# A hybrid decoder step on one core: forget rows stacked in one strip and made in the convolution, queries padded earlier, modulation pieces in every second unit

## The chip, the cores and the metric

The kernel runs on one core of a Trainium2 chip. The metric is the device time of one execution in microseconds. Times of single instructions come from one profiled execution; they count from its first instruction.

## What is computed

One layer of a decoder for two groups: a prompt of 512 tokens and 8 running samples (one token each, 2048 past positions in a paged cache). From the reference, cut to what matters here:

```python
mod = silu(c) @ w_mod + b_mod                       # 6 x 1024 columns, for 9 rows c
sh1, sc1, g1, sh2, sc2, g2 = split(mod, 6)
h = rms(x) * (1 + sc1) + sh1
gq, gk, gv, gz, ga, gb, fq, fk, fv, ff = split(h @ w_in)
# gated delta: short causal convolution of gq, gk, gv, silu, chunked state update -> o_gdn
# forgetting attention, 8 heads x 64:
F = cumsum(log_sigmoid(ff + fox_fb))
s = q @ k.T * 64 ** -0.5 + F[q] - F[k]              # causal; samples: over cached pages too
o_fox = softmax(s) @ v
x = x + g1 * (concat(o_gdn, o_fox) @ w_out)
x = x + g2 * peer(rms(x) * (1 + sc2) + sh2)         # 16 of 16384 experts for each of 8 heads
y = rms(x) * final_norm_w
```

## The kernel before

All engines run programs of their own that meet at semaphores. The stages, with their times in the profile: the first four of twelve chunks of `w_mod` (to 80 us), the input projections (to 205), the convolution (205 to 290), the forgetting attention of the prompt in **units** (307 to 462), the first tile's gated-delta levels with the output projection (to 600), and the expert part (to the end), in which POOL gathers rows of `peer_uv`.

**Projections and keys.** Weight chunks of 2 MB go through a ring; from the fourth chunk on only two slots alternate. SP issues all loads and stores in one order that is written out by hand. `chunk(n)` waits for the last matmul of the chunk that had the slot before. Beside the projections, POOL multiplies the samples' cached keys with their queries (`key_product`, line 2291), in 32 groups of 1 MB, and DVE reduces them (`key_group`).

**The convolution** (lines 625 to 643). PE makes twelve blocks in three groups `gq`, `gk`, `gv`; ACT, DVE and PE turn each block back (`conv_back`). After the last, PE makes the forget rows: `forget_rows(i)` multiplies `LOGF` with triangles into a bank, 1, 2, 4 and 7 matmuls for the four tiles, and ACT (lines 1182 to 1187) copies them into four strips `FORGET[i]`, rows 0 to 7, that lie in `MV` and in `HT`. Then PE turns the tails of the convolution (`TAILI`, to DVE's `TAILO`) and the samples' log forget pages (`forget_turns`), and DVE makes the score of the samples' new key.

**Padding the queries.** Two heads share 128 partitions. `FQ` keeps the even heads and `FQO` the odd ones, the other 64 partitions zero. On POOL, behind the 32 key products, stand in this order: `sample_conv(0)` (the samples' convolution of one group, 7 steps on 8x512), two memsets of the strips, the copy of 64 partitions into `FQO`, two memsets of 64 partitions, then `sample_conv(1)` and `sample_conv(2)`. PE's unit 0 waits for all five of the strips' and queries' instructions.

**Units.** There are 34 steps u, for 8 heads x 4 query tiles. Unit u has on PE `fox_scores(u)` (three matmuls: keys, forget row spread by a column of `ident`, mask), `fox_turn(u - 1)`, `fox_values(u - 2)`; on DVE the maximum (1649), a copy (1657) and the scaling (1666); on ACT the exponential (1204). In chosen units stands more, from tables by unit:

- `MOD_AT = (2, 5, 8, 12, 15, 18, 21, 24)`: `mod_chunk` on PE (64 matmuls on a chunk of the ring) and `mod_row` on DVE (line 1483, four instructions).
- PE's `steps` and DVE's `between`: the forget sums of the pages (`forget_sums`, unit 1; `forget_after` with 15 additions on line 1738 and one on 1740), `sample_scores` (units 9; lines 1747, 1749, 1752), the softmax of the samples (units 10 to 17), the samples' delta state (`srule_...`, units 16, 19, 22, 25, 29, with long instructions on lines 1692, 1699 and 1705 and three products on POOL between them).
- From unit 18 on one group of cached values each (`sample_values(n)`, n = u - 18): four pages of 256 KB, in a rotation of three buffers.
- After unit 10 ACT applies SiLU to the samples' convolution (line 1208), which waits for all three of POOL's `sample_conv`.

**SP's order around the units** (lines 2498 to 2590). `sconv_load(0)`, chunk 11 (the fifth modulation chunk), `sconv_load(1)`, chunk 12, `sconv_load(2)`; each `sconv_load(g)` waits for `sample_conv(g - 1)`. Then the biases of pieces 4 and 5, the stores of the convolution's tails, the samples' new score and two loads. Then `next_mod(m)` for m = 4, 5, 6: it waits for the piece's rows, stores them, loads a bias and issues the chunk after next (m + 9). Then it waits for the SiLU of unit 10, stores its result, loads the samples' state, and goes through the steps z of `for z in range(LEVELS_END)`: `next_mod` at z = MOD_AT + 2 for the remaining pieces, and `value_pages(n)` three steps ahead of its use:

```python
numbers = page_numbers(n)          # four register loads, line 2439
...
cache_group("cache_v", 32 + n, numbers)
```

## Time and profile before

| | |
|---|---|
| median of 3 runs | 2075.9 us (2069.58 to 2078.93) |
| the profiled execution | 2079.02 us, its span 2077.1 us |
| mean granted clock of TensorE | 0.916 |
| busy: PE, DVE, ACT, POOL | 80%, 65%, 32%, 39% of the span |
| HBM read | 718.50 MB, 350 GB/s over the span |
| DMA share from 640 us to the end | 0.99 |

The busy shares are means over stages that differ. Which engine or queue sets the end has to be read from the stage in question: from the windows, then from the chain of waits, then from the timeline of the engine that the chain names. Line numbers in rows are those of the kernel before; 484 and 491 are PE's helpers for matmul and transpose, 2380 and 2385 are SP's for loads and stores, and 2439 is the read of a page number into a register.

### The profile page before, as it was taken

The numbers are of one execution on the slowest core, as the hardware profiler recorded it, in microseconds if no ns is written. First come the engines' busy times: TensorE is split into PE (matmuls) and PEld (weight loads), VectorE is DVE, ScalarE is ACT, GpSimd is POOL, SyncE is SP. The second block draws the span as 40 slices with busy tenths as digits, with TensorE's granted clock in tenths as the row PEclk, the third lists the DMA queues.
The fourth block names the chain that finished last, engine by engine and source line by source line (L and its number), as shares of the span: only waits on it lengthen the run. The fifth ranks groups of instructions, "written<-read, shape, count | busy, mean of one in ns | idle before, by whom it ended". The sixth has DMA issues, their size and how long they took to land.

```text
span 2077.1 us, 25939 instructions
## 1 busy us (share of the span) xinstructions
PE 1654.9 (80%) x8212; PEld 880.5 (42%) x8212; DVE 1353.7 (65%) x3075; ACT 669.0 (32%) x1956; POOL 809.3 (39%) x604
## 2 busy tenths in 40 slices
PE   6999988888887896766599676759978778977776
PEld 4546546546664453333255234325522443322232
DVE  4236866564458886756878665688857667676754
ACT  2111222211124453323345332344523333442332
POOL 0178672213004443334354343434424344444441
PEclk9999999887998998999799899989978998999999
DMA  8378645886579999999999999999999999999996
GB/s 297 108 256 278 230 151 153 308 280 207 170 261 414 404 415 414 413 414 421 411 378 420 414 414 414 421 409 390 421 392 352 417 419 392 422 422 422 421 417 284
DMA packets 168826, 729.20 MB, mean 351 GB/s; under 512 B 17622, under 2 KB 18471, under 8 KB 101987
## 3 DMA queue, kind: packets, MB, share of 16 engines
q0 software_dynamic: 75024, 545.82, 64.0%
q1 hardware_dynamic: 93666, 181.73, 25.4%
q8 instruction: 67, 1.10, 0.2%
q14 instruction: 69, 0.56, 0.1%
HBM read 718.50 MB, written 9.09 MB: 350 GB/s over the span
## 4 chain that ended last, share of the span: by engine, by line
PE 36%; DMA 30%; DVE 12%; issue 8%; POOL 6%; SPq 4%; ACT 4%; DVEq 0%; POOLq 0%; ACTq 0%
PE bank L484 35%; DMA R<-in_peer_uv,R 21%; DMA R<-in_w_out 4%; POOL MV L2291 3%; SPq L2380 3%; DVE R L2127 2%; DVE RING L2127 2%; DMA RING<-in_peer_uv,R 2%; DMA R<-in_peer_wq 2%; POOL R L2291 1%; SPq L2439 1%; ACT R L1348 1%; PE bank L491 1%; POOL R L2366 1%; DVE R L1912 1%
## 5 line engine op out<-in xcount | busy, mean ns | idle before, releaser
L2366 POOL DMA_INDIRECT RING<-in_peer_uv,R x390 | 439.9, 1128 | 712.6 <-PE bank L484 577.3
L484 PE MATMUL bank<-RING,R 128*64 128x512 f32 (+2 forms) x1560 | 514.8, 666 | 223.7 <-ACT R L1348 219.8
L2127 DVE SCALAR_TENSOR_TENSOR RING<-RING,MV 128x1024 f32<-128x1024 f32 x288 | 351.5, 1223 | 177.9 <-DMA RING<-in_peer_uv,R 169.1
L484 PE MATMUL bank<-R 128*128 128x128 f32 (+6 forms) x2216 | 396.7, 375 | 83.1 <-ACT R L1348 75.1
L484 PEld LDWEIGHTS bank<-R 128*128 128x128 f32 (+3 forms) x2216 | 260.7, 186 | 243.3 <-issue 235.7
L484 PEld LDWEIGHTS bank<-RING,R 128*64 128x64 f32 (+2 forms) x1560 | 156.4, 159 | 484.5 <-issue 472.5
L1358 ACT ACTIVATE R<-R 128x2 f32<-128x2 f32 x256 | 51.8, 202 | 716.0 <-DVE RING L2127 592.8
L2366 POOL DMA_INDIRECT R<-in_peer_uv,R x130 | 147.6, 1136 | 213.8 <-PE bank L484 196.8
L2127 DVE SCALAR_TENSOR_TENSOR R<-R,MV 128x1024 f32<-128x1024 f32 x96 | 117.6, 1225 | 58.0 <-DMA R<-in_peer_uv,R 56.5
L2127 DVE SCALAR_TENSOR_TENSOR RING<-RING,R 128x1024 f32<-128x1024 f32 x96 | 117.3, 1222 | 55.1 <-DMA RING<-in_peer_uv,R 50.6
L484 PEld LDWEIGHTS bank<-HT,R 128*128 128x128 f32 x1024 | 128.0, 202 | 56.3 <-issue 55.2
L484 PE MATMUL bank<-HT,R 128*128 128x128 f32 (+1 forms) x1024 | 139.2, 293 | 5.5 <-DMA R<-in_peer_wq 4.7
L484 PE MATMUL bank<-HT,RING 128*128 128x512 f32 x320 | 141.6, 600 | 0.0
L2291 POOL TENSOR_TENSOR MV<-MV,RING 128x2048 f32<-128x2048 f32 x22 | 99.3, 4528 | 89.5 <-DMA RING<-samp_d 56.6
L1365 ACT ACTIVATE R<-R 128x1 f32<-128x1 f32 x512 | 122.8, 287 | 8.4
L484 PE MATMUL bank<-R,HT 128*128 128x64 f32 (+4 forms) x320 | 103.8, 461 | 22.1 <-DMA R<-in_w_out 22.1
L484 PE MATMUL bank<-RING,HT 128*8 128x128 f32 (+5 forms) x768 | 106.7, 345 | 5.1 <-ACT HT L1098 3.7
L1348 ACT ACTIVATE R<-hide_q,R 128x64 f32<-128x64 f32 x384 | 109.7, 333 | 0.0
L484 PE MATMUL bank<-R,ident 128*128 128x512 f32 (+3 forms) x228 | 99.3, 537 | 0.1
L484 PEld LDWEIGHTS bank<-HT,RING 128*128 128x128 f32 x320 | 60.7, 193 | 72.4 <-issue 72.3
L484 PEld LDWEIGHTS bank<-RING,HT 128*8 128x8 f32 (+1 forms) x768 | 63.4, 139 | 45.5 <-issue 43.9
L484 PEld LDWEIGHTS bank<-R,HT 128*128 128x128 f32 (+1 forms) x320 | 49.0, 199 | 77.6 <-issue 74.5
(322 smaller groups left out, 1842.3 us busy)
## 6 DMA issues: line engine op xcount, KB each, us to landing
R<-in_peer_wq SPq DMA_DIRECT2D x16, 2048.0 KB, 28.6
RING<-in_w_mod SPq DMA_DIRECT2D x12, 2048.0 KB, 8.3
MV<-in_cache_k SPq DMA_DIRECT2D x88, 256.0 KB, 3.5
R<-in_cache_v SPq DMA_DIRECT2D x84, 256.0 KB, 3.7
R<-in_w_out SPq DMA_DIRECT2D x6, 2048.0 KB, 34.4
MV<-in_cache_v SPq DMA_DIRECT2D x44, 256.0 KB, 4.0
RING<-in_w_in SPq DMA_DIRECT2D x5, 2048.0 KB, 9.7
R<-in_cache_k SPq DMA_DIRECT2D x40, 256.0 KB, 3.7
```

Source lines behind the costliest of these rows:

```text
L484: i = nc.tensor.matmul(out, lhsT, rhs, start=start, stop=stop, **k)
L491: i = nc.tensor.transpose(out, in_, ident[0:n, 0:n])
L1348: A(dst[:, k % 4, :], ones_, ACT.Copy, scale=AG[:, n % 4, s_:s_ + 1]).then_inc(S("diagonal"), 1)
L1358: A(AG[:, n % 4, s_:s_ + 2], DOT[:, n % 4, s_:s_ + 2], ACT.Gelu).then_inc(S("gelu"), 1)
L1365: A(AG[:, n % 4, x:x + 1], AG[:, n % 4, x:x + 1], ACT.Copy, scale=gate).then_inc(S("weights"), 1)
L1912: V.tensor_tensor(M, AT, level[:, lv:lv + 1, :].to_broadcast([P, 4, P]), ALU.mult).then_inc(S(f"level{hb}"), 1)
L2127: V.scalar_tensor_tensor(u, u, 1.0, H2HIGH if s_ % 2 and n < PAIRED * PH else H2[n // PH % 2], ALU.mult, ALU.mult, accum_out=DOT[:, n % 4, ...
L2291: T(k, k, QB[:, n // 4 % 2:n // 4 % 2 + 1, :].to_broadcast([P, 4, 512]), ALU.mult).then_inc(S("kprod"), 1)
L2366: nc.gpsimd.indirect_dma_start(UV[g % UN], None, a["peer_uv"][0], bass.IndirectOffsetOnAxis(ap=idx, axis=0)).then_inc(S(f"uv_in{g % UN}"), 16)
L2380: sp.dma_start(dst, src, **k).then_inc(S(sem), 16)
L2439: return [sp.value_load(PTB[0:1, 4 * n + g:4 * n + g + 1], min_val=0, max_val=a["cache_k"].shape[1] - 1) for g in range(4)]
```

## The change

`FORGET` becomes one strip of 512 columns in `R2`; tile i has its eight rows at partitions 32 i to 32 i + 7, and the matmul that spreads them takes column 32 i + h of `ident`. POOL zeroes the strip at the very start. `PR`, which had that place, moves to the start of `HT`. `forget_rows` and the ACT copies move behind the group `gk`, inside the convolution. The copy of the odd queries moves from POOL to ACT, behind the last SiLU; POOL's two memsets of queries stand ahead of `sample_conv(0)`. The tails, the turn of the log forget pages, the new score and the forget sums' additions become entries of the tables, in units 0 to 8. The modulation pieces stand in units 1, 3, ..., 15. SP's order follows: chunk 12 ahead of `sconv_load(1)`, two groups of value pages ahead of piece 6, pieces 4 to 8 ahead of the wait for unit 10's SiLU.

```diff
-        FORGET = [MV[:, 2, 256:384], HFLAT[:, 256:512], MV[:, 2, 384:768], HFLAT[:, 512:1024]]
+        FORGET = R2[:, 8192:8704]
-        PR = part(R2, 8192, 1024, n=2, c=512)
+        PR = part(HFLAT, 0, 1024, n=2, c=512)
-        MOD_AT = (2, 5, 8, 12, 15, 18, 21, 24)
+        MOD_AT = (1, 3, 5, 7, 9, 11, 13, 15)
 # PE
                 if g == 0:
                     decay_sums()
+                if g == 1:
+                    for i in range(TILES):
+                        forget_rows(i)
             conv_back(10)
             conv_back(11)
-            for i in range(TILES):
-                forget_rows(i)
-            (tails turned here)
-            forget_turns()
-                    pe.wait_ge(S("fox_zero"), 5)
+                    pe.wait_ge(S("fox_zero"), 2)
-                mm(b[:, 0:w], ident[:, h:h + 1].to_broadcast([P, P]), FORGET[i][:, 0:w], False, False)
+                mm(b[:, 0:w], ident[:, 32 * i + h:32 * i + h + 1].to_broadcast([P, P]), FORGET[:, 0:w], False, False)
-            steps = {1: forget_sums, 10: sample_max_turn, 12: sample_max_spread, 16: sample_sums}
+            steps = {0: tail_turns, 1: forget_turns, 3: forget_sums, 10: sample_max_turn, 12: sample_max_spread, 16: sample_sums}
 # ACT, at g == 1, behind the three exponentials
+                    act.wait_ge(S("forget_cleared"), 1)
+                    for i in range(TILES):
+                        b = full_bank(act, ("frow", i))
+                        rows = slice(32 * i, 32 * i + 8)
+                        if i:
+                            A(FORGET[rows, 0:i * P], b[0:8, 0:i * P], ACT.Copy).then_inc(S("forget_cols"), 1)
+                            act.wait_ge(S("forget_cols"), i)
+                        A(FORGET[rows, i * P:(i + 1) * P], b[0:8, i * P:(i + 1) * P], ACT.Copy, scale=-1.0).then_inc(free(("frow", i)), 1)
             conv_silu(11)
+            A(FQO[64:P, :, :], FQ[64:P, :, :], ACT.Copy).then_inc(S("odd_queries"), 1)
             act.sem_inc(S("sample_ready"), 1)
-            (the copies of the forget rows)
 # DVE
-            between = {1: forget_after, 9: sample_scores, ...}
+            between = {0: tails_out, 1: forget_turned, 2: new_scores, 3: forget_after, 4: lambda: forget_pages(14, 12), 5: lambda: forget_pages(11, 9),
+                       6: lambda: forget_pages(8, 5), 7: lambda: forget_pages(4, 0), 8: forget_total, 9: sample_scores, ...}
 # POOL
+            nc.gpsimd.memset(FORGET, 0.0).then_inc(S("forget_cleared"), 1)
 ...
             for n_ in range(32):
                 key_product(n_)
+            job_done(pool, ("gv", 4))
+            pool.wait_ge(S("kprod"), 32)
+            nc.gpsimd.memset(FQO[0:64, :, :], 0.0).then_inc(S("fox_zero"), 1)
+            pool.wait_ge(S("odd_queries"), 1)
+            pool.wait_ge(S("fox_zero"), 1)
+            nc.gpsimd.memset(FQ[64:P, :, :], 0.0).then_inc(S("fox_zero"), 1)
+            pool.wait_ge(S("fox_zero"), 2)
             sample_conv(0)
-            (two memsets of strips, the copy and two memsets of queries)
             sample_conv(1)
             sample_conv(2)
 # SP
             sconv_load(0)
             chunk(11)
-            sconv_load(1)
             chunk(12)
-            sconv_load(2)
             sp.wait_ge(S("kred"), 32)
             bmod(4)
             bmod(5)
+            sconv_load(1)
 ...
+            next_mod(4)
             sp.wait_ge(S("new_score"), 1)
 ...
-            for m in range(4, 7):
+            next_mod(5)
+            sconv_load(2)
+            for n in range(2):
+                cache_group("cache_v", 32 + n, page_numbers(n))
+            for m in range(6, 9):
                 next_mod(m)
 ...
-                if z - 2 in MOD_AT[3:]:
+                if z - 2 in MOD_AT[5:]:
```

## Rows read from the trace of the kernel before

**Rows 1.** Windows by stage: PE, PEld, DVE, ACT, POOL busy, clock, DMA share, GB/s

```profile
205.00:290.00 85.00, 85.00 (x406) 42.12 (x408) 65.98 (x77) 25.06 (x56) 49.55 (x12) 1.00 0.62 201
...
367.00:450.00 83.00, 68.27 (x587) 43.53 (x579) 50.14 (x101) 13.91 (x37) 21.15 (x3) 0.86 0.91 315
...
450.00:640.00 190.00, 152.41 (x960) 113.47 (x957) 92.07 (x206) 39.51 (x77) 30.05 (x25) 0.84 0.66 230
...
640.00:2077.00 1437.00, 1108.02 (x4665) 531.31 (x4663) 1010.55 (x2472) 540.28 (x1677) 577.39 (x510) 0.92 0.99 405
```

**Rows 2.** The chain of waits from 280 to 440 us

```profile
by line: SPq L2380 20.2%; issue 15.2%; SPq L2439 14.0%; PE bank L484 11.5%; SPq L2385 5.9%; POOL MV L2291 5.7%; DMA R<-in_cache_v 4.4%; PE bank L491 3.9%; DVE RING L1738 3.8%; POOL R L2299 2.4%; POOL R L2300 2.4%; DVE RING L1740 1.4%; ACT R
...
352.37 1.49 ACT R L1208
...
382.67 0.39 SPq L2380
```

**Rows 3.** The timeline around the last convolution, POOL then PE; start, duration

```profile
291.02 1.26 POOL L2297 TENSOR_TENSOR R<-R 8x512 f32<-8x512 f32 x1
...
300.50 0.53 POOL L2308 MEMSET MV<- 128x512 f32 x1 [0.22 <-POOL R L2300]
...
305.65 1.80 POOL L2316 MEMSET R<- 64x2048 f32 x1
...
307.55 0.46 PE L484 MATMUL bank<-R 128*128 128x128 f32 x2 [2.58 <-issue]
```

**Rows 4.** The timeline there, ACT and PE

```profile
291.77 0.63 ACT L1159 ACTIVATE R<-R 128x512 f32<-128x512 f32 x1 [0.25 <-ACT R L1117]
...
293.04 0.39 PE L484 MATMUL bank<-upper,small 128*8 128x128 f32 x2
...
293.26 0.38 PE L484 MATMUL bank<-lower,small 128*8 128x128 f32 x2
```

**Rows 5.** SP's timeline, 308 to 441 us

```profile
316.88 0.68 SPq L2380 DMA_DIRECT2D R<-in_state_conv  x1
...
374.42 1.89 SPq L2380 DMA_DIRECT2D R<-in_cache_v  x4
...
376.35 1.44 SPq L2385 DMA_DIRECT2D mod_d<-MV  x4
...
379.27 0.40 SPq L2380 DMA_DIRECT2D RING<-in_w_mod  x1
...
431.96 2.00 SPq L2380 DMA_DIRECT2D R<-in_cache_v  x4
```

**Rows 6.** SP's instructions of line 2439; ns min/median/max

```profile
L2439 SPq TENSOR_LOAD <-RQ x64: 260/266/1261, 366.9 to 451.3; - x64
```

**Rows 7.** DMA issues in three windows; last number: median us to landing

```profile
RING<-in_w_mod SPq DMA_DIRECT2D x8, 2048.0 KB, 8.2
...
R<-in_cache_v SPq DMA_DIRECT2D x4, 256.0 KB, 3.4
...
R<-in_cache_v SPq DMA_DIRECT2D x4, 256.0 KB, 6.3
```

**Rows 8.** PE's timeline, 360 to 445 us

```profile
366.87 1.93 PE L484 MATMUL bank<-RING,small 128*9 128x128 f32 x64
...
440.73 1.94 PE L484 MATMUL bank<-R,RING 128*32 128x512 f32 x8 [4.14 <-DMA R<-in_cache_v]
```

**Rows 9.** DVE: line 1738 (ns min/median/max), then its timeline

```profile
L1738 DVE TENSOR_TENSOR RING<-RING x15: 267/275/1362, 316.0 to 321.0; 128x64 f32<-128x64 f32 x15
...
346.04 1.22 DVE L1747 TENSOR_TENSOR RING<-RING 128x1024 f32<-128x1024 f32 x1
...
403.05 7.12 DVE L1692 TENSOR_REDUCE R<-R 64x64 f32<-64x4096 f32 x1
...
420.32 4.47 DVE L1699 SCALAR_TENSOR_TENSOR R<-R,small 64x4096 f32<-64x4096 f32 x1
...
436.82 7.04 DVE L1705 TENSOR_REDUCE R<-R 64x64 f32<-64x4096 f32 x1
```

More of the change, by code:

```diff
@@ L635, in _, with tail_turns @@
                     decay_sums()
+                if g == 1:
+                    for i in range(TILES):
+                        forget_rows(i)
             conv_back(10)
             conv_back(11)
-            for i in range(TILES):
-                forget_rows(i)
-            pe.wait_ge(S("tails"), 12)
-            for q in range(3):
-                b = take_bank(("tail", q), "D")
-                for j in range(4):
-                    tr(b[0:3, j * P:(j + 1) * P], TAILI[:, q * 4 + j, :], full(("tail", q)) if j == 3 else None)
+            def tail_turns():
+                pe.wait_ge(S("tails"), 12)
+                for q in range(3):
+                    b = take_bank(("tail", q), "D")
+                    for j in range(4):
+                        tr(b[0:3, j * P:(j + 1) * P], TAILI[:, q * 4 + j, :], full(("tail", q)) if j == 3 else None)
             def forget_turns():
@@ L1632, in _, with tails_out, new_scores @@
             conv_tokens(11)
-            for q in range(3):
-                b = full_bank(dve, ("tail", q))
-                V.tensor_copy(TAILO[0:3, q * 512:(q + 1) * 512], b[0:3, :]).then_inc(S("tail_out"), 1)
-                dve.wait_ge(S("tail_out"), q + 1)
-                dve.sem_inc(free(("tail", q)), 1)
-            dve.wait_ge(S("sample_ready"), 1)
-            T8 = CACC[0:NB, 0, :]
-            dve.wait_ge(S("decays"), 3)
-            step(V.scalar_tensor_tensor(small[:, 786:818], small[:, 300:332], -1.0, small[:, 690:722], ALU.mult, ALU.mult))
-            step(V.tensor_tensor(T8, PS[0:NB, COL_FQ:COL_FQ + 512], PS[0:NB, COL_FK:COL_FK + 512], ALU.mult))
-            settle()
-            V.tensor_reduce(SN[0:NB, :], T8.rearrange("p (h d) -> p h d", h=8), AXX, ALU.add).then_inc(S("new_score"), 1)
+            def tails_out():
+                for q in range(3):
+                    b = full_bank(dve, ("tail", q))
+                    V.tensor_copy(TAILO[0:3, q * 512:(q + 1) * 512], b[0:3, :]).then_inc(S("tail_out"), 1)
+                    dve.wait_ge(S("tail_out"), q + 1)
+                    dve.sem_inc(free(("tail", q)), 1)
+            def new_scores():
+                dve.wait_ge(S("sample_ready"), 1)
+                T8 = CACC[0:NB, 0, :]
+                dve.wait_ge(S("decays"), 3)
+                step(V.scalar_tensor_tensor(small[:, 786:818], small[:, 300:332], -1.0, small[:, 690:722], ALU.mult, ALU.mult))
+                step(V.tensor_tensor(T8, PS[0:NB, COL_FQ:COL_FQ + 512], PS[0:NB, COL_FK:COL_FK + 512], ALU.mult))
+                settle()
+                V.tensor_reduce(SN[0:NB, :], T8.rearrange("p (h d) -> p h d", h=8), AXX, ALU.add).then_inc(S("new_score"), 1)
             def fox_max(u):
@@ L1736, in forget_after, with forget_pages, forget_total @@
                     job_read(dve, ("ltot", half))
-                for g in range(14, -1, -1):
+            def forget_pages(last, first):
+                for g in range(last, first - 1, -1):
+                    settle()
                     step(V.tensor_tensor(TP[:, :, :, g], TP[:, :, :, g], TP[:, :, :, g + 1], ALU.add))
-                    settle()
+            def forget_total():
+                settle()
                 step(V.tensor_tensor(flat(LP[:, :, :, 0:15]), flat(LP[:, :, :, 0:15]), flat(TP[:, :, :, 1:16]), ALU.add))
@@ L2512, in _, with next_mod @@
             store(o["conv_prompt"][0, 0], TAILO[0:3, :], "samples_out")
+            def next_mod(m):
+                mod_store(m)
+                if m + 2 < 12:
+                    bmod(m + 2)
+                chunk(m + 9)
+            next_mod(4)
             sp.wait_ge(S("new_score"), 1)
@@ L2552, in value_pages @@
                 b, q = divmod(n, 4)
-                numbers = page_numbers(n)
+                if n >= 2:
+                    numbers = page_numbers(n)
                 if buffer_of(32 + n) == 3 and group_before(32 + n) is None:
@@ L2558, in value_pages @@
                     sp.wait_ge(S("values_read"), before_ - 32 + 1)
-                cache_group("cache_v", 32 + n, numbers)
+                if n >= 2:
+                    cache_group("cache_v", 32 + n, numbers)
                 if q == 0:
```

27 lines of the change are left out of this document (1 added, 26 removed).

## The prediction

> **What bounds the kernel now.** I read the busy time by stage first [rows 1]. The last 1437 us, from 640 on, have a DMA share of 0.99 at 405 GB/s: expert rows and weights stream there and nothing in the change touches them, so a gain made earlier is handed down whole and no more. In the convolution (205 to 290) PE is busy all 85 us at full clock (1.00, the 2.4 GHz level). In the units of forgetting attention neither PE nor DVE is full (68 and 50 of 83 us from 367 on, clock 0.86) [rows 1], so something else sets the pace there.
>
> The chain of waits names it [rows 2]: SP's own instructions are the largest part between 280 and 440 (20.2% and 14.0% for the two lines that issue loads and read page numbers). It enters SP from the SiLU of the samples' convolution, which ACT does in unit 10 and ends at 353.9; from there SP issues without a pause to speak of up to the pages of unit 29, issued at 431.96 [rows 5], for which PE then waits until 440.73 [rows 8]. The kernel's middle is thus a serial list of SP. The way into it is the second thing to look at: POOL works 9.3 us on the first sample convolution, then until 307.45 on zeroing and copying, and unit 0 starts only at 307.55 [rows 3].
>
> **Part 1, the start of the units.** The forget rows move into the convolution. Pairs of passes start 0.22 us apart at full clock (293.04, 293.26) [rows 4]; 14 pairs are 3.1 us on an engine that is full, so the convolution ends at 293.4 in place of 290.3. The seven small ACT copies fall into gaps of some 6 us that ACT has there and cost nothing; without those gaps they would cost 0.3 us each. The last SiLU moves from 291.77 [rows 4] to 294.9 and ends at 295.5. Behind it stands ACT's new copy of half the queries, 64x2048. No such instruction exists before: a floor is ACT's 8x1536 at 1.49 us [rows 2], a ceiling is POOL's 64x2048 memset at 1.80 [rows 3] scaled up by a third; both say 1.5 to 2.4, I take 1.9, as 1.49 grows to 1.98 with the length. To 297.4, then POOL's second memset, 1.80, to 299.2. The first runs beside ACT. Unit 0 starts at 299.4: **8.2 us earlier**. The turns of the tails and of the forget pages now stand behind scores in units 0 and 1, in the shadow of waits for ACT's first table.
>
> **Part 2, what SP must do before the SiLU.** POOL's first sample convolution, in front of the queries before, is now behind them: 299.2 to 308.5. SP stands at the second group's load for exactly that. Its list from there, from its own rows [rows 5, 6]: the load of state and weights, 0.68 for the first of its two DMAs, 1.2 in all; three stores at the same rate, 1.6; the first modulation piece, stores, bias and chunk, 3.3 as from 376.35 to 379.67, to 314.6; the new score's store, some 2 of waiting for it (an estimate, not below 1 and not above 3) and two loads, 3.8; second piece 3.3 to 321.6; wait for POOL's second group to 323, load 1.2; two groups of value pages, each four register loads of 0.27 plus 0.15 and a gap, 2.6 together, and 1.89 of issues: 9.0, to 333.2; third and fourth piece 6.4, to 339.6. A chunk of 2 MB lands 8.2 us after its issue [rows 7]. The piece of unit 5 (issued 314.2, landed 322.4) costs 1 or 2 us, that of unit 7 none, but that of **unit 9** is issued at 336.0 and lands at 344.2, where PE could have been there at 336. PE's 1.93 [rows 8], DVE's rows to 347.5, then the three passes of sample scores (1.22 each, 3.8) [rows 9], the maximum, the exponential, ACT's table and SiLU of 2.8: it ends at **355.5 against 353.9**. The 8.2 us of the earlier start are eaten by SP's list.
>
> **Part 3, from the SiLU to the pages.** SP's stores and state loads are as before, 9.4, then one piece, 3.3: chunk issued at 367.7, landed 375.9, used in unit 15. Piece 10 (1.85, no bias any more) fits below it. PE arrives in unit 15 at 366 and waits till 375.9; its rows are done at 379.1, SP's last piece to 381, page numbers 2.6: the third group of values is issued at 383.6 against 382.67 before [rows 2]. So here the change is 1 us **behind**. What it gained, two groups out of the list (9.0) and two pieces, went into the wait for that chunk.
>
> **Part 4, behind unit 20.** Before, three pieces stood among the nine page groups from 382.67 to 431.96 [rows 2, 5]: 3.3, and 1.85 for each of the two without a bias, together 7.0. Now none: 9 x 4.5 + 0.7 = 41.2 against 49.3, so the group of unit 29 is issued at 424.8, 7.2 earlier. It also lands sooner: behind a chunk a group takes 6.3 from issue to landing, alone 3.4 [rows 7]. PE gets it at 430 in place of 440.73. PE and DVE now come into play: nine units with values are about 33 us of PE, and of DVE's state reduction of 7.1 in unit 22 and update of 4.5 in unit 25 [rows 9] some 7 stick out, as PE's gaps around them do now, so 432 to 433. **Net 8 us less.** Unit 30, the rest of the units, the levels and the gather stage follow it; the page groups of the levels wait on values read and move along.
>
> **Sum:** -8 us at the end of the units, against the profiled execution's own 2079.02: 2071. The median shown, 2075.9, lies 3.1 below that execution, so for the median I say 2075.9 - 8 = 2068. This main case has its own range of -3 to -13: the 1.5 to 2.4 of the copy, the landing times (7.8 to 9 us a chunk), and PE's clock, which is 0.84 in the stretch from 450 on [rows 1], after waits, and may do so after the new ones in units 9 and 15. A measurement of this kernel can tell about 0.5%, 10.4 us, from no change.
>
> **POOL beside DVE.** The forget sums' 15 additions are 0.275 us at the median but 1.362 at most [rows 9]; the long ones are those beside one of POOL's passes of 1.26 [rows 3]. Before they fell into a gap of POOL's; in units 4 to 8 they lie beside its second and third sample convolution. The Trainium skill (SBUF - State Buffer, Who interferes with whom) says that a DVE instruction with two SBUF inputs blocks against a GpSimd one that reads SBUF, whole instruction against whole instruction; the trace agrees. By it all 15 would take the long form. By the rows that is 15 x 1.09 = 16 us more on DVE, against none; I take half, since POOL rests between its groups, and put it under the wait for the chunk of unit 9, where DVE has 8 us. If all of it came, some 5 us would stick out and the main case would be -3. That is a rival of its own with 0.08.
>
> **Rivals.** *The front holds its gain* (0.22): SP reaches the chunk of unit 9 early enough, say because POOL's groups end sooner. The SiLU then ends near 343, and all shifts by a further 12: -20, 2056. For it: SP stands behind POOL at both loads, before (the one at 316.88 [rows 5] follows the end of POOL's second group at once) and after, so whatever POOL gains counts. Against it: the sum of SP's rows leaves it 1.6 us of waiting only.
>
> *The back is not SP's* (0.12), the slower side. The samples' state chain is a ladder of DVE and POOL steps tied to the units 16 to 32, with DVE's long ones at 403.05, 420.32 and 436.82 [rows 9]. From unit 15's piece (366.87 [rows 8]) to the end of the last of them, 443.9, it takes 77 us. The piece now waits for its chunk until 375.9, 9 later. If the 77 us stay, because the ladder and not the pages paced the units, unit 29 ends at 453, and with 3 of doubled collisions the kernel is +12: 2088. It decides if unit 15's piece to the end of unit 29's reduction still takes over 70 us. Against it: the three long DVE steps are 18.6 us of it, and PE's largest single waits are for value pages.
>
> *The change does nothing* (0.08): each gain is met by the next wait, within 2 us. The ring of two slots would then be the rate all through.
>
> **How the numbers follow.** Main case 0.50, of which a fifth lies beyond -10.4; the front's gain 0.22; nothing 0.08; collisions 0.08; the ladder 0.12, three quarters of it beyond +10.4. Faster: 0.10 + 0.22 = 0.32, rounded up to 0.33, as the front may win in part. Slower 0.09. Same 0.58. The range reaches from the front's gain, 2056, to a little over the case of nothing, 2079; what is left out is the ladder and the tail of the front.
>
> **What would show it.** Unit 0's scores at 299.4; a PE wait for a w_mod load of some 8 us in unit 9 and of 10 in unit 15; the SiLU's end near 355; third value group at 383.6; PE's wait in unit 29 for cached values, 4.14 us before [rows 8], gone or short; no piece on SP behind 381. Wrong if those ring waits are absent (front) or if the 77 us from unit 15 to unit 29 stay (ladder).

## The result and the profile after

The changed kernel takes 2085.1 us (median of 20 runs, 2077.8 to 2096.1), the kernel before 2076.8 (20 runs, 2068.9 to 2086.3). The ratio is 1.0037 with an interval of 1.0024 to 1.0050: slower by 0.4%, within the 0.5% that the prediction called no change, but outside its range, which ended at 2079, and on the other side of the forecast of 8 us less. The profiled execution spans 2084.5 us, 7.4 more than that of before. Three executions far above all others, one each of the kernel before (2173.9), e3_pieces_old (2364.8) and e6_no_chunks (5161.5), stand in no ratio.

The windows by stage (columns as in [rows 1]) show where to look:

```profile
205.00:290.00 85.00, 84.67 (x367) 42.05 (x366) 59.23 (x69) 23.17 (x55) 47.66 (x12) 1.00 0.60 193
299.00:308.00 9.00, 9.00 (x97) 7.26 (x98) 5.11 (x12) 2.31 (x5) 8.53 (x7) 0.68 0.15 52
308.00:367.00 59.00, 42.26 (x471) 31.55 (x470) 37.77 (x93) 10.45 (x23) 17.87 (x15) 0.86 0.68 226
367.00:450.00 83.00, 67.29 (x501) 44.20 (x499) 50.07 (x100) 15.82 (x42) 21.14 (x3) 0.94 0.79 258
```

For the stretch from 308 to 367 the kernel before has this row:

```profile
308.00:367.00 59.00, 48.78 (x472) 37.28 (x473) 38.96 (x100) 15.23 (x35) 17.91 (x14) 0.91 0.51 157
```

PE is busy all 9 us from 299 to 308 (6.25 of them before). Then it loses 6.5 us of busy time in the next 59, while the DMAs move more (226 GB/s against 157). So the start is earned and then lost. PE's timeline says at which instructions (start, duration, wait before it and what ended it):

```profile
299.00 0.77 PE L484 MATMUL bank<-R 128*128 128x128 f32 x2 [3.19 <-issue]
...
322.09 1.94 PE L484 MATMUL bank<-RING,small 128*9 128x128 f32 x64
...
336.09 3.28 PE L484 MATMUL bank<-RING,small 128*9 128x128 f32 x64 [7.25 <-DMA RING<-in_w_mod]
...
347.56 0.47 PE L491 MATMUL bank<-ident,HT 128*128 128x128 f32 x1 [5.13 <-ACT HT L1209]
...
349.56 3.37 PE L484 MATMUL bank<-RING,small 128*9 128x128 f32 x64
...
384.00 3.21 PE L484 MATMUL bank<-RING,small 128*9 128x128 f32 x64 [5.38 <-DMA RING<-in_w_mod]
```

The pieces are the rows with `RING,small`. Those of units 5, 7, 9 and 15 stand here. The one of unit 7 waits 7.25 us for its chunk and that of unit 15 waits 5.38. Both then take 3.2 to 3.3 us instead of 1.94, at a granted clock of 0.56 and 0.58 (1.00 for the piece of unit 5). The piece of unit 9 takes 3.4 us, behind PE's wait of 5.13 for ACT.

SP's timeline shows why the chunk of unit 7 was late:

```profile
314.36 0.40 SPq L2393 DMA_DIRECT2D RING<-in_w_mod  x1
314.82 0.45 SPq L2398 DMA_DIRECT2D sgate_d<-RQ  x1
...
322.14 0.36 SPq L2393 DMA_DIRECT2D RQ<-out_logf_sample  x1
...
326.35 0.39 SPq L2393 DMA_DIRECT2D RING<-in_w_mod  x1
326.78 0.70 SPq L2393 DMA_DIRECT2D R<-in_state_conv  x1
...
339.98 0.40 SPq L2393 DMA_DIRECT2D RING<-in_w_mod  x1
343.64 0.40 SPq L2393 DMA_DIRECT2D RING<-in_w_mod  x1
...
375.96 0.52 SPq L2393 DMA_DIRECT2D RING<-in_w_mod  x1
...
392.99 2.00 SPq L2393 DMA_DIRECT2D R<-in_cache_v  x4
...
433.78 1.93 SPq L2393 DMA_DIRECT2D R<-in_cache_v  x4
```

The chain of waits shows how long the chunk of unit 7 then took to land:

```profile
326.35 9.70 DMA RING<-in_w_mod
```

SP's waits from 290 to 460 (total, times, longest) give the same list by cause:

```profile
SPq L2398 <- DVE MV L1488: 19.4, 4, 10.2
SPq L2393 <- DMA sgate_d<-RQ: 6.8, 1, 6.8
```

The first is SP waiting for the rows of a piece (`MV`). They wait for PE, and PE waits for the chunk, so a delay goes round. But not all of it is the ring's: ahead of unit 9's piece PE waits 5.13 us for ACT, which comes behind five additions of the forget sums on DVE (5.81 us). The second is the store of the new score, 0.2 KB, issued at 314.82 right behind the 2 MB of the chunk at 314.36.

The chain of waits from 280 to 440, by line, has turned over against [rows 2]:

```profile
by line: PE bank L484 52.5%; DMA RING<-in_w_mod 11.1%; PE bank L491 7.4%; issue 5.6%; DVE R L1702 4.4%; DVE MV L1488 4.2%; DVE RING L1752 2.8%; DVE R L1709 2.2%; DVE HT L1667 0.9%; DVE RING L1791 0.8%; DVE RING L1779 0.8%; DVE RQ L1785 0.8%
```

SP's issues and register loads, a third of the chain before, are gone from it. In their place stand PE and the loads of `w_mod`. The SiLU and the last long step of DVE:

```profile
360.95 1.48 ACT L1213 ACTIVATE R<-R 8x1536 f32<-8x1536 f32 x1
...
442.64 7.09 DVE L1715 TENSOR_REDUCE R<-R 64x64 f32<-64x4096 f32 x1
```

The SiLU ends at 362.4 (353.9 before), the third value group is issued at 392.99 (382.67, both [rows 2]), the reduction of unit 29 starts at 442.64 (436.82 [rows 9]). At the end of the units DVE's first memset of the levels marks the time, before, then after:

```profile
460.48 0.48 DVE L1843 MEMSET R<- 128x512 f32 x1 [0.35 <-DVE R L1809]
```

```profile
464.12 0.48 DVE L1861 MEMSET R<- 128x512 f32 x1 [0.35 <-DVE R L1826]
```

The loss of 10.3 us at 393 has shrunk to 3.6 there. The first expert gather is issued at 623.78 against 618.53.

### The profile page after: what moved, and what is told of

Its sections match the earlier page's. It is cut to its first block, busy times and chain, and to the rows that moved or that the text cites. A ratio compares the mean times of both kernels' runs of the same rounds, so it can differ in the third digit from the quotient of the medians.

```text
span 2084.5 us, 25938 instructions
## 1 busy us (share of the span) xinstructions
PE 1667.9 (80%) x8212; PEld 881.3 (42%) x8212; DVE 1348.2 (65%) x3075; ACT 670.8 (32%) x1957; POOL 805.8 (39%) x602
## 4 chain that ended last, share of the span: by engine, by line
PE 46%; DMA 29%; DVE 15%; issue 4%; ACT 4%; POOL 1%; SPq 1%; DVEq 0%; ACTq 0%; POOLq 0%
PE bank L484 44%; DMA R<-in_peer_uv,R 17%; DMA R<-in_w_out 6%; DMA RING<-in_peer_uv,R 5%; DVE RING L2145 3%; DVE R L2145 2%; DMA RING<-in_w_mod 2%; PE bank L491 2%; ACT R L1353 1%; SPq L2393 1%; POOL R L2379 1%; DVE R L1930 1%; ACT R L1363 1%; ACT R L1370 0%; DVE R L1919 0%
## 5 line engine op out<-in xcount | busy, mean ns | idle before, releaser
L484 PE MATMUL bank<-R 128*128 128x128 f32 (+6 forms) x2216 | 406.3, 382 | 87.6 <-ACT R L1353 78.0
L484 PE MATMUL bank<-R,ident 128*128 128x512 f32 (+5 forms) x292 | 125.1, 526 | 0.1
```

Of the source, the lines that this page charges most:

```text
L484: i = nc.tensor.matmul(out, lhsT, rhs, start=start, stop=stop, **k)
```

## The experiments

All ratios are to the kernel before, on the same chip and in the same hours: over 20 runs of each for the change, and over 7 to 12 runs against 18 to 35 of the kernel before for the others. The landmarks are those of one profiled execution of each kernel. "Units' end" is the start of the memset just named. The times of the landmarks:

| kernel | ratio (interval) | SiLU ends | third value group | units' end | first gather |
|---|---|---|---|---|---|
| before | 1 | 353.9 | 382.7 | 460.5 | 618.5 |
| the change | 1.0037 (1.0024 to 1.0050) | 362.4 | 393.0 | 464.1 | 623.8 |
| e1_store_first | 1.0013 (0.9994 to 1.0033) | 360.9 | 392.5 | 463.9 | 620.6 |
| e2_pages_in_loop | 1.0028 (1.0010 to 1.0047) | 362.3 | 393.3 | 467.6 | 620.4 |
| e3_pieces_old | 0.9954 (0.9935 to 0.9974) | 348.2 | 373.3 | 450.4 | 601.1 |
| e4_adds_by_6 | 1.0024 (1.0007 to 1.0042) | 362.1 | 393.3 | 464.6 | 621.2 |
| e5_small_first | 0.9930 (0.9906 to 0.9954) | 347.9 | 371.0 | 450.1 | 600.5 |
| e6_no_chunks | 0.9936 (0.9911 to 0.9961) | 354.2 | 380.0 | 450.5 | 607.2 |
| e7_old_pages_in_loop | 0.9971 (0.9952 to 0.9990) | 349.6 | 378.4 | 458.1 | 609.3 |
| e8_mid_pieces | 0.9977 (0.9958 to 0.9996) | 355.9 | 376.1 | 459.2 | 619.7 |
| e9_small_adds | 0.9962 (0.9943 to 0.9981) | 349.8 | 375.0 | 452.8 | 606.3 |
| e10_conv_first | 0.9973 (0.9956 to 0.9991) | 355.2 | 377.8 | 457.6 | 615.2 |
| e11_old_store_first | 0.9967 (0.9949 to 0.9984) | 349.7 | 374.1 | 453.8 | 604.4 |
| e12_small_again | 0.9953 (0.9933 to 0.9972) | 347.7 | 370.9 | 449.6 | 607.3 |

**e1_store_first.** The new score's store and its two loads go ahead of piece 4's chunk.

```diff
-            next_mod(4)
             sp.wait_ge(S("new_score"), 1)
...
+            next_mod(4)
             next_mod(5)
```

> Edit: the changed kernel, with SP's fifth modulation piece (its row stores, bias and 2 MB chunk) moved from ahead of the new score's store to behind the two loads that wait for that store. In the changed kernel SP stands 6.8 us for this store, which was issued 0.4 us behind the chunk. Theory 1 (SP's list and the queue order starve the ring): the wait falls to some 2 us, the next chunk is issued near 321.5 instead of 326.35, PE's wait of 7.3 us in unit 7 shrinks to under 3, the SiLU of unit 10 ends near 357 instead of 362.4, and the time falls by 3 to 6 us against the changed kernel (about 2080, ratio to the kernel before 1.001). Theory 2 (the units are longer because PE and DVE have more work in each, the ring is incidental): the SiLU stays within 1.5 us of 362.4 and the time does not move. Theory 3 (DVE's additions beside POOL): POOL's third group starts near 327 instead of 337 and the additions of unit 7 escape it, so part of the gain is that.

Measured: 2082.6 us against 2079.3. The wait of 6.8 is down to 0.3. But two chunks are now issued in a row, at 317.85 and 321.46, with the loads of `sample_conv` and eight value pages behind them, and they take 9.0 and 11.7 us to land. PE pays one piece earlier, in unit 5:

```profile
326.86 3.60 PE L484 MATMUL bank<-RING,small 128*9 128x128 f32 x64 [4.93 <-DMA RING<-in_w_mod]
336.01 1.94 PE L484 MATMUL bank<-RING,small 128*9 128x128 f32 x64
```

The piece of unit 7 starts at 336.01 against 336.09, the SiLU ends 1.5 us sooner, the third group is issued 0.5 sooner. The ratio, 1.0013, is what the first theory said (1.001), 0.24% below that of the change, but the intervals overlap, and the landmarks do not bear the theory out: the SiLU was to end at 357 and ends at 360.9, and the units end where they did (463.9 against 464.1). The small store's wait is real; up to the end of the units it cost this kernel next to nothing, since the chunks, and DVE's additions beside POOL (5.17 us for four of them here), take its place.

**e2_pages_in_loop.** The two value groups that the change issues early go back into the loop over the steps.

```diff
-            for n in range(2):
-                cache_group("cache_v", 32 + n, page_numbers(n))
...
-                if n >= 2:
-                    numbers = page_numbers(n)
+                numbers = page_numbers(n)
```

> Edit: the changed kernel, with the first two groups of cached values back in the loop of the units instead of between the sixth and seventh piece on SP. Theory 1: SP's list ahead of unit 9 is shorter by 8.8 us, and the chunk of unit 7 lands in 8 instead of 9.7 us, so unit 9's piece comes 3 to 6 us earlier and so does the SiLU (357 to 359), but 9 us of page reads and issues return behind it; they fall into the wait for the chunk of unit 15, which is 10.2 us on SP, so the third group is issued 3 to 5 us earlier than 393.0: 2 to 5 us faster than the changed kernel. Theory 2: nothing in front moves and the 9 us on SP behind come on top or are hidden: same or slower by up to 5.

Measured: 1.0028, no difference that the intervals show. The SiLU ends at 362.3, where it did; PE's waits for chunks stay (7.46 and 5.27 in units 7 and 15) and one of 2.43 for values comes back. SP's list ahead of the SiLU got 9 us shorter and the SiLU did not move. The lines show why. The chunk of unit 9 is issued at 330.80, 9.2 us sooner, and takes 12.4 us to land, yet its piece starts where it did, behind five of DVE's additions that stand beside POOL's third convolution (SP, DVE, PE):

```profile
330.80 0.39 SPq L2393 DMA_DIRECT2D RING<-in_w_mod  x1
```

```profile
340.74 5.92 DVE L1752 TENSOR_TENSOR RING<-RING 128x64 f32<-128x64 f32 x5
```

```profile
349.58 3.25 PE L484 MATMUL bank<-RING,small 128*9 128x128 f32 x64
```

So this run does not show that SP's list costs nothing here; it shows that something else ended at the same time. And at the end of the units this kernel stands 3.5 us behind the change (467.6 against 464.1), which the ratio doesn't show.

**e3_pieces_old.** The pieces stand in the units of before, the rest of the change stays.

```diff
-        MOD_AT = (1, 3, 5, 7, 9, 11, 13, 15)
+        MOD_AT = (2, 5, 8, 12, 15, 18, 21, 24)
...
-            for m in range(6, 9):
+            for m in range(6, 7):
...
-                if z - 2 in MOD_AT[5:]:
+                if z - 2 in MOD_AT[3:]:
```

> Edit: the changed kernel, with the modulation pieces in the units of the kernel before (2, 5, 8, 12, 15, 18, 21, 24) and SP's pieces placed to match; forget rows, padding, spread tables and the early value pages stay. Theory 1: the ring does not starve the units any more, unit 10 starts near 335 to 338, the SiLU ends at 343 to 348 (POOL's third group is then the bound), the third value group is issued near 368 to 375, and the kernel is 8 to 15 us faster than the changed one and 2 to 8 faster than the one before (ratio 0.996 to 0.999). Theory 2 (work in each unit decides): unit 10 moves by the two or three pieces fewer ahead of it, 3.2 us each, so by 6 to 7 us, and the back gets them again: within 3 us of the changed kernel.

Measured: 2069.4 against 2079.3, a ratio 0.8% below that of the change. No wait for `w_mod` is left on PE from 300 to 400; its list there is this:

```profile
PE bank L491 <- ACT HT L1209: 7.6, 3, 6.1
PE bank L484 <- DMA R<-in_cache_v: 5.2, 1, 5.2
PE bank L484 <- issue: 3.2, 1, 3.2
```

The SiLU ends at 348.2, 14 us before that of the change, though SP still waits 6.9 for the small store:

```profile
SPq L2398 <- ACT R L1213: 7.0, 1, 7.0
SPq L2393 <- DMA sgate_d<-RQ: 6.9, 1, 6.9
```

The five additions that took 5.81 us in the change take 1.50: they are over before POOL's third convolution starts. The units end at 450.4, 13.7 us before those of the change and 10 before those of the kernel before. And SP's two lines are again the largest part of the chain from 280 to 440, as in [rows 2]:

```profile
by line: SPq L2393 17.7%; PE bank L484 14.6%; SPq L2452 11.5%; issue 10.1%; DMA R<-in_conv_w 5.6%; SPq L2398 5.2%; POOL R L2318 4.8%; POOL R L2319 4.8%; DMA sgate_d<-RQ 4.7%; DMA R<-in_cache_v 4.5%; DMA MV<-in_cache_k 3.7%; POOL MV L2310 2.
```

So the piece move costs more than all the rest of the change gains: at the end of the units 13.7 us against 10.1.

**e4_adds_by_6.** The last five additions of the forget sums and their total move from units 7 and 8 to unit 6, away from POOL's third convolution.

```diff
-                       6: lambda: forget_pages(8, 5), 7: lambda: forget_pages(4, 0), 8: forget_total, 9: sample_scores,
+                       6: lambda: (forget_pages(8, 0), forget_total()), 9: sample_scores,
```

> Edit: the changed kernel, with the last five of the 15 additions and the total moved from units 7 and 8 to unit 6, where DVE and POOL are idle while PE waits for the chunk of unit 7. Theory 3 (DVE's additions blocked by POOL's passes cost the units): the 5.81 us that five additions took in unit 7 become about 1.5 in unit 6 and are hidden, PE's wait of 5.1 us in unit 9 for ACT goes, the piece of unit 9 then waits for its chunk if that has not landed (issued 339.98, about 349), so PE gains at most 1 or 2 us there and the SiLU ends at 360 to 362; the time falls by 0 to 2 us. If it falls by 4 or more, the collision was the bound and not the chunk.

Measured: the nine additions take 2.71 us, 0.30 each. In the change the first four of the last five take 4.47 us, 1.12 each:

```profile
340.83 4.47 DVE L1752 TENSOR_TENSOR RING<-RING 128x64 f32<-128x64 f32 x4
```

The time stays: SiLU at 362.1, units' end 464.6, ratio 1.0024. In place of the long additions PE waits for the chunk of unit 9:

```profile
349.01 3.60 PE L484 MATMUL bank<-RING,small 128*9 128x128 f32 x64 [5.00 <-DMA RING<-in_w_mod]
```

The collision is real, and in the change it and the chunk of unit 9 hid each other: without the additions the chunk holds the piece until 349.01, and without the late issue (e2) the additions hold it until 349.58. A kernel with both edits was not run, so what the two cost together stays open. (The Trainium skill, SBUF - State Buffer, Who interferes with whom, has DVE and GpSimd exclude each other on a shared port pair; the trace agrees for those that fall beside POOL's passes, and in the change that is 5 of 15.)

**e5_small_first.** e3 with both small transfers ahead of the chunks: the new score's store and loads ahead of piece 4's, the third group's convolution load ahead of piece 5's.

```diff
             sp.wait_ge(S("new_score"), 1)
...
+            next_mod(4)
+            sconv_load(2)
             next_mod(5)
-            sconv_load(2)
```

> Edit: the kernel with the pieces in the old units (e3_pieces_old), and SP's small transfers put ahead of its 2 MB chunks: the new score's store and its two loads ahead of piece 4, the third group of the samples' convolution ahead of piece 5. In e3_pieces_old SP stood 6.9 us for the score's store, 0.4 us behind a chunk in the same queue, and the third group's load took 9 us to land, so POOL started it at 337.25 and ACT's SiLU in unit 10 waited 5.4 us for it. If small transfers wait in the queue behind large ones: the wait for the store is about 2 us, POOL's third group starts near 325 to 328, the SiLU ends at 340 to 344 instead of 348.2, and the kernel is 3 to 7 us faster than e3_pieces_old (ratio to the kernel before 0.992 to 0.994). If the queue's order is not it (stores of scattered rows are slow by themselves): the wait stays at 6 to 7 us and the time with it.

Measured: 2061.8 against 2080.0. The ratio is what was expected, the way to it is not: POOL's third group starts at 328.6 instead of 337.3, but the SiLU ends at 347.9 and not at 340 to 344. The third value group is issued 2.3 us sooner, and the units end where they did (450.1 against 450.4). POOL now works beside the additions of unit 7, which take 5.83 us. So the step to 0.993 has no counterpart before the end of the units, and the repetition below does not confirm it.

**e6_no_chunks.** The change, but the chunks of pieces 6 to 11 are not loaded: these pieces multiply with what the slots hold. It leaves out 12 MB of reads and computes those six pieces of the modulation from old weights. The places, SP's stores and biases and PE's matmuls stay.

```diff
+        LEFT_OUT = range(13, 19)
...
+                if n in LEFT_OUT:
+                    return
```

> Edit: the changed kernel with six of its twelve w_mod chunks (those of pieces 6 to 11) not loaded; these pieces multiply what the two slots hold from pieces 4 and 5, so their outputs differ, and 12 MB less are read. All matmuls, rows, stores and waits else stay. Theory 1 (the ring starves the units): PE's waits of 7.3, about 5 and 5.4 us for w_mod in units 7, 9 and 15 are gone, unit 10 starts before 345 (352 before), the SiLU ends at 345 to 352 instead of 362.4, the third value group is issued before 378 instead of at 393.0, and the time is 10 to 18 us below the changed kernel. Theory 2 (pieces in every second unit are too much work for PE and DVE): less than 4 us.

Measured: 2067.8 against 2080.0. No piece waits for a chunk; in the trace that of unit 7 starts at 330.80 and that of unit 15 at 371.56, 12.4 us before that of the change. The units end at 450.5, as in e3. With the chunks free the dense places cost nothing by the end of the units, although DVE's additions are long here too (2.95 us for three, 5.19 for four). So the loads cost the 14 us, and not PE's and DVE's work in the dense units. What of the loads it is, the landing, SP's waits for a free slot or the 12 MB in the queue, this run does not separate; the new score's store goes free with them, since the chunk ahead of it is one of the six. e3, which loads all of them, reaches the same end.

**e7_old_pages_in_loop.** e3 and e2 together: pieces at their old places and no early value groups (the edits stand above).

> Edit: the pieces in the old units (e3_pieces_old), and the two early groups of cached values back in the loop. With sparse pieces SP has time ahead of the SiLU (it waits 7.0 us for it in e3_pieces_old), so the early groups were free there, and now cost 9 us on SP's list behind it. If SP's list paces the units from the SiLU to unit 29, the third group is issued 6 to 9 us later than the 373.3 of e3_pieces_old and the kernel is 5 to 9 us slower than it (ratio to the kernel before 0.999 to 1.001). If PE and DVE pace these units: within 2 us of e3_pieces_old.

Measured: 2072.3 against 2080.0. The SiLU stays (349.6), the third group is issued at 378.4 instead of 373.3, PE waits 5.4 and 5.2 us for values, and the units end 7.7 us later than in e3. The early value groups bring that here, and 3.5 us in e2. The medians differ by less, and their intervals overlap (0.9971 and 0.9954).

**e8_mid_pieces.** e5 with the pieces between the two sets of places.

```diff
-        MOD_AT = (2, 5, 8, 12, 15, 18, 21, 24)
+        MOD_AT = (1, 3, 6, 8, 11, 13, 16, 18)
...
-            for m in range(6, 7):
+            for m in range(6, 8):
...
-                if z - 2 in MOD_AT[3:]:
+                if z - 2 in MOD_AT[4:]:
```

> Edit: e5_small_first with the pieces in units 1, 3, 6, 8, 11, 13, 16, 18, so that four of the eight are issued ahead of the SiLU and only two stand among the page groups. If a chunk needs about 8 us to land plus 5 of SP, PE and DVE around it, units 6, 8 and 11 wait 0 to 2 us each, the SiLU ends within 3 us of that of e5_small_first, and with two pieces fewer among the page groups the time is 0 to 5 us below it. If the ring starves again (waits for w_mod of over 3 us in two or more units), it is slower than e5_small_first by 2 to 8.

Measured: 2075.6 against 2080.0. PE waits 4.11 us for the chunk of unit 6, whose piece starts at 327.45, and 2.28 in unit 16; the units end at 459.2, 9 us behind e5. In these three traces the cost grows with the density: the units end at 450, 459 and 464 for the three sets of places, though the last has the small transfers in the other order.

**e9_small_adds.** e5 with the additions of e4, to have small transfers first and no collision.

```diff
-                       6: lambda: forget_pages(8, 5), 7: lambda: forget_pages(4, 0), 8: forget_total, 9: sample_scores,
+                       6: lambda: (forget_pages(8, 0), forget_total()), 9: sample_scores,
```

> Edit: e5_small_first, with the last five additions and the total of the forget pages moved to unit 6, as in e4_adds_by_6. In e5_small_first POOL's third group started 9 us earlier (328.56), and five additions that now fell beside it took 5.83 us in place of 1.50, so the SiLU ended at 347.9, no earlier. If these collisions took what the earlier group gave: the additions take under 4 us for all nine, before 330, unit 9 is 3 to 5 us earlier, the SiLU ends at 341 to 345 and the kernel is 1 to 5 us faster than e5_small_first (ratio 0.990 to 0.993). If something else holds unit 10: the SiLU stays at 347 to 348 and the time too. SP's list then starts earlier, and PE's and DVE's own pace may take part of it back behind.

Measured: 2069.4 against 2079.2, not faster than e5: a miss. Nine additions in one unit take 3.65 us and their total 2.19 beside POOL's passes (1.15 in the change), the next unit's maximum stands behind them on DVE, and PE has its longest wait of the stretch there, then runs slow:

```profile
334.75 1.12 PE L491 MATMUL bank<-ident,HT 128*128 128x128 f32 x4 [5.62 <-ACT HT L1209]
336.98 2.47 PE L484 MATMUL bank<-RING,small 128*9 128x128 f32 x64
...
354.21 3.60 PE L484 MATMUL bank<-RING,small 128*9 128x128 f32 x64
```

In e5 the longest such wait there, at 336.10, is 2.12 us, and both pieces take 1.94. The units end 2.7 us later. Gathering DVE's work shortened one collision, moved another onto the total and made a longer block.

**e10_conv_first.** e9 with POOL's first sample convolution back ahead of the padding of the queries.

```diff
+            sample_conv(0)
             (the two memsets of queries)
-            sample_conv(0)
```

> Edit: e9_small_adds, with the first sample convolution on POOL back ahead of the padding of the queries, where the kernel before has it. It ends 5 us earlier, but unit 0 starts at 307.5 to 309 instead of 299.3. If the start of the units is what the end inherits (SP's list and the rest just follow it): unit 10 and the SiLU are 5 to 8 us later than in e9_small_adds and so is the time. If SP's list ahead of unit 10 is the bound there: the list starts at 304 instead of 308.7, and the SiLU stays within 2 us of that of e9_small_adds, and so does the time.

Measured: 2073.4 against 2079.2. PE's first unit starts at 308.42 instead of 300.13, as in the kernel before, the SiLU ends at 355.2, the units at 457.6: 4.9 us behind e9. Of the 8.3 us of the earlier start 4.9 arrive at the end of the units of these two traces, once the pieces are sparse; the medians (0.9973 and 0.9962) do not tell the two apart.

**e11_old_store_first and e12_small_again.** e11 is e5 with the third group's convolution load behind piece 5's chunk again; e12 is the kernel of e5 once more.

```diff
             next_mod(4)
-            sconv_load(2)
             next_mod(5)
+            sconv_load(2)
```

> The pieces at the old places, with only the new score's store and loads ahead of piece 4's 2 MB chunk; the third group's load of the samples' convolution is behind chunk 5 again. It tells the two small transfers apart. If the small store is the one that counts, the store's wait of 6.9 is gone and the time is that of the kernel with both moved, 0.993 within 0.002. If the third group's load counts, POOL's third group starts near 334 and no earlier, and the time lies near the kernel with neither moved, 0.995.

> The kernel of the fastest run so far, the same file on another occasion. If its 0.993 was its own, it comes again at 0.991 to 0.996, with POOL's third group starting near 328.5 and the third value group issued near 371. If it was a lucky set of runs, it comes with the others that have the old places of the pieces, at 0.996 or above.

Measured: e11 2071.5 and e12 2068.4, against 2076.1. POOL's third group starts at 338.73 in e11 and at 328.39 in e12; the units end at 453.8 and 449.6. The kernel of e5 comes at 0.9953 here after 0.9930, so no difference between e3, e5 and e11 is shown. What remains sure is that all of them are faster than the kernel before, by 0.3 to 0.7% with the old places of the pieces.

The two executions of the one kernel also show where such scatter can sit. At the landmarks up to the end of the units they agree within 0.5 us. Their first gathers are issued at 600.5 and 607.3. The stretch from 450 to 480 in e5, then in e12 (columns as above, the clock third from the end):

```profile
450.00:480.00 30.00, 21.96 (x130) 13.68 (x129) 14.06 (x19) 6.26 (x9) 9.24 (x7) 0.82 0.62 196
```

```profile
450.00:480.00 30.00, 24.25 (x115) 17.89 (x115) 12.20 (x18) 5.77 (x8) 8.37 (x6) 0.65 0.52 160
```

and PE's first two long groups of passes of the levels in each:

```profile
455.56 2.05 PE L484 MATMUL bank<-R 64*128 64x128 f32 x16
458.63 2.05 PE L484 MATMUL bank<-R 64*128 64x128 f32 x16
```

```profile
456.80 3.78 PE L484 MATMUL bank<-R 64*128 64x128 f32 x16
462.51 3.78 PE L484 MATMUL bank<-R 64*128 64x128 f32 x16
```

The same passes run at 2.4 GHz in one (granted clock 1.00 over them) and at 1.2 in the other (0.50), behind waits of PE for DVE of 2.11 us and 2.18 us, so nearly the same. One of DVE's steps behind them starts at 463.30 and at 467.27: 4.0 of the 7 us have arisen by there. In both profiled executions of this case's pair the passes take 3.78 (clock 0.72 from 450 to 480 before, 0.75 after). From the end of the units to the gather all these profiles lie between 150 and 161 us, and one kernel alone gives 150.5 and 157.7, so the end of the units is the landmark to compare single executions by.

## Why the prediction was wrong

**Part 1 held.** Unit 0 starts at 299.00 (299.4 said). ACT's new copy takes 1.91 us (1.9 said), POOL's memset behind it 1.80, its first convolution starts at 298.98:

```profile
295.13 1.91 ACT L1191 ACTIVATE HT<-R 64x2048 f32<-64x2048 f32 x1
...
297.10 1.80 POOL L2329 MEMSET R<- 64x2048 f32 x1 [0.99 <-ACT HT L1191]
...
298.98 1.25 POOL L2316 TENSOR_TENSOR R<-R 8x512 f32<-8x512 f32 x1
```

The 8 us of the start were there.

**Part 2 failed.** It said of the ring: "The piece of unit 5 (issued 314.2, landed 322.4) costs 1 or 2 us, that of unit 7 none", and it put the first long wait in unit 9. The wait is in unit 7, 7.25 us. Three terms were small: the new score's store, "some 2 of waiting for it" and "not above 3", took 6.8, since it stood behind 2 MB in the queue; the chunk took 9.7 us to land, not 8.2; and a piece after a wait takes 3.3 us, not 1.93, at the lower clock. The SiLU ended at 362.4 instead of 355.5.

Unit 9 then handed this on. The forecast had its chunk issued at 336.0 and landed at 344.2; it was issued at 339.98, took 8.5 us, and the piece started at 349.56 and took 1.4 us more than 1.93. These 5.4 and 1.4 us make up the SiLU's 6.9 but for 0.1.

e1 shows that the store alone does not explain it. With it mended the chunks stood closer together and landed later, and the SiLU came 1.5 us sooner, not 5. The error lies in the way of adding, too: Part 2 added up SP's list and priced the ring only where that list arrived late at it. But SP's list, PE's piece, DVE's rows and the landing form a circle over two slots, in which the delay of one is handed to the others. From the first piece (305.14) to the eighth (384.00) the pieces start 11.3 us apart on the mean (7.6 to 14.0); without the loads (e6) they start 9.5 apart. Only fewer pieces in the stretch (e3) or chunks that need no landing (e6) brought the end of the units forward by much, both by 14; a shorter list of SP (e1, e2) or fewer long additions of DVE (e4) brought it no more than 0.3 us. These three edits were each run alone, and e2 and e4 show that the list and the additions cover each other at unit 9. So it is shown that the loads in dense places cost the 14 us, and not shown that they would with a short list and short additions together. Of the two ring waits that the prediction named as its signs, that of unit 15 is there (5.38 us, 10 said), and that of unit 9 stands in unit 7.

**Part 3** foresaw that the change would stand behind at the third value group, by 1 us; it stands 10.3 behind (392.99, where 383.6 was said). 6.9 of the 9.4 us between these two are the SiLU's, from Part 2; the chunk of unit 15, on the way, was issued at 375.96 instead of 367.7.

**Part 4 held in kind.** The group of unit 29 is issued at 433.78, 40.8 us behind the third (41.2 said). PE's wait for values in unit 29 ([rows 8], 4.14 us) is gone. But the units' end regained 6.7 us and not 9. From 367 to 460 PE no longer waits for values (13.5 us before) but 5.8 us for DVE's products of the samples' values (line 1798 of the changed kernel, 1.3 for the same line before), 4.4 of it at once. That DVE held the rest back was not tested.

The sum then: -8 said at the end of the units, +3.6 measured. The front gives 9.4 of the miss of 11.6, the back 2.3. The rest up to the 8.3 of the medians arises behind the units; of it 1.6 stands at the first gather, and two executions of one kernel differ there by 6.8, so it is not read further.

**What was not asked.** The forecast weighed the change against the kernel before as a whole. It gave the piece move the 7 us of three pieces out of the page groups, and saw its price only as a delay that eats a gain. The parts alone are another picture: without the piece move the change gives -10 us at the end of the units (e3) and 0.9954 in all; with it, +3.6. The question what the change would be with the pieces left where they were would have put the two side by side, and with it the ring as the thing to price.

**The rivals.** *The front holds its gain* (0.22) was refuted for the change, and it is what e3 does in half: the SiLU ends at 348.2 there, 5.7 us before that of the kernel before (the rival said 343). *The back is not SP's* (0.12) gave the right side with the wrong mechanism. Its own test, from unit 15's piece to the end of unit 29's reduction, gives 384.00 to 449.73, 65.7 us, not over 70. *The change does nothing* (0.08), "the ring of two slots would then be the rate all through", comes nearest to what the runs showed, that the loads in dense places eat the gain (e3, e6). A fixed rate is not shown, as the pieces start 7.6 to 14.0 us apart, and its size was set at nothing within 2 us, without a price for the slower passes behind a wait. *Collisions* (0.08) fell on 5 of the 15 additions, 4.3 us more than five take in e3; removing them alone gained nothing (e4), as the chunk of unit 9 was no earlier, and what they cost beside a shorter list of SP was not run. The range reached only a little over this case, so its own width upwards is what was missing.

**The best version** that was run is the change with the pieces in their old units (e3, e5, e11, e12): 0.993 to 0.997 of the kernel before. The medians lie 4.6 to 18.3 us below it, 10 on the mean of the four.

## What to carry to other kernels

Work that needs a transfer each time has a circle time (issue, landing, use, release, and who issues the next); divide the stretch by the number of turns before making its places denser, and price what PE loses in clock behind each wait. Where two delays end at the same time, taking away either one alone shows nothing; both have to go in one run before one of them is called free. Where a change bundles moves, estimate each one alone against the kernel before: a gain in one can hide the loss of another. And in one queue a small transfer on which a next step waits belongs ahead of the large ones.

## What the runs showed of the hardware

A store of 0.2 KB issued on SP's queue 0.5 us behind a 2 MB load kept SP waiting 6.8 to 6.9 us (the change, e3, e4). With the store ahead of the load (e1) or the load left out (e6) SP waits 0.3 and 0.8 us: the transfer that waits for the store is issued 0.9 us behind the end of the store's own issue. (The Trainium skill, DMA: Bandwidth & Descriptors, Queues, rings and completion order, says that a transfer's semaphore increment lands only after every earlier write of the same DMA engine; these three cases agree with it.) The samples' convolution load, issued right behind a chunk until 328.03, let POOL go at 337.25 in the change, 9.2 us later.

A piece of 64 matmuls takes 1.94 us, or 3.2 to 3.6 behind a wait of 2.3 to 7.7 us for its chunk (the change, e1, e2, e4, e8; granted clock 0.50 to 0.58 where it was read, in the change and e8, against 1.00). The levels' passes take 2.05 or 3.78 us in two executions of one kernel that stood within 0.5 us of each other at the end of the units and had waited 2.11 and 2.18 us just before.

DVE's additions of 128x64 take 0.30 us each away from POOL's passes (1.50 us for five in e3) and 1.12 to 1.18 beside them (4.47 us for four, 5.81 and 5.92 for five in the change and e2).
